# Between dilated attention and the RWKV recurrence: low-rank weights loaded with the constants, last statistics in three PSUM banks, memsets moved, first key norm ahead of the scan

## The reference

```python
for g, (window, dilation) in enumerate(((128, 1), (512, 4), (2048, 16))):
    num, den, mx = dilated_group_attention(q[g], k[g], v[g], ...)   # unnormalised
m_all = max(maxes); wts = [exp(mx - m_all) for mx in maxes]
o_attn = sum(w * n) / sum(w * d)                  # 8 heads of 64
y_attn = (o_attn * silu(z_attn)) @ w_up_attn
pr = pr + (pr_prev - pr) * shift_mix              # r, k, v, w_low, a_low
w_log = -softplus(-(w0 + tanh(w_low) @ w_up)) - 0.5
a = sigmoid(a0 + a_low @ a_up)
kk = k * k_k; kk = kk / max(norm(kk), 1e-12)      # per head: the key norm
k = k * (1 + (a - 1) * k_a)
y = rwkv7_scan(r, exp(-exp(w_log)), k, v, -kk, kk * a)
bonus = sum(r * k * r_k) * v
```

## Time and profile before

| | us |
|---|---|
| median of 3 runs | 2829.97 (2827.18 to 2830.27) |
| profiled execution | 2842.01 |
| span of the profiled execution | 2840.2 |
| TensorE matmuls busy | 2707.1 (95% of the span) |
| VectorE busy | 1264.2 (45%) |
| ScalarE busy | 810.1 (29%) |
| GpSimd busy | 1040.2 (37%) |

### The profile page before, as it was taken

How to read it: one execution, slowest core, us unless ns; L and a number is a source line. 1 busy time by engine, 2 the same in 40 slices (tenths; PEclk the granted TensorE clock), 3 DMA queues, 4 the chain that set the end, 5 groups by cost and what they waited for, 6 DMA issues and landing times.

```text
span 2840.2 us, 44277 instructions
## 1 busy us (share of the span) xinstructions
PE 2707.1 (95%) x17968; PEld 2176.6 (77%) x17968; DVE 1264.2 (45%) x2338; ACT 810.1 (29%) x1607; POOL 1040.2 (37%) x1318
## 2 busy tenths in 40 slices
PE   6999999997999999999898999999998998999999
PEld 5787777875867777686787888788887887777777
DVE  4225252435847466484531433533335003377743
ACT  3444444444113131220212211211113003255531
POOL 2223232232322231321455133344444456435442
PEclk9999999998999999999998899999999996999999
DMA  3111111111101010111331211111111121111122
GB/s 125 41 45 41 42 45 49 45 45 38 35 17 55 28 49 28 34 46 61 152 119 61 74 45 46 43 45 45 45 45 38 52 67 56 45 38 45 43 109 84
DMA packets 200907, 154.02 MB, mean 54 GB/s; under 512 B 5120, under 2 KB 183680, under 8 KB 200064
## 3 DMA queue, kind: packets, MB, share of 16 engines
q1 hardware_dynamic: 186256, 106.44, 12.6%
q10 hardware_dynamic: 14448, 44.74, 4.1%
HBM read 128.10 MB, written 23.07 MB: 53 GB/s over the span
## 4 chain that ended last, share of the span: by engine, by line
PE 79%; DVE 12%; ACT 6%; issue 1%; POOL 1%; DMA 1%; ACTq 0%; DVEq 0%; SPq 0%; POOLq 0%
PE gemm L527 21%; PE gemm L529 19%; PE gemm L528 19%; ACT prob L1942 3%; DVE neg_logits L1488 2%; DVE prob L1503 2%; PE scores L578 1%; PE scores L769 1%; PE weighted L829 1%; PE weighted L605 1%; PE probs_t L766 1%; PE probs_t L590 1%; PE scores L904 1%; PE scores L758 1%; DVE stats L1492 1%
## 5 line engine op out<-in xcount | busy, mean ns | idle before, releaser
L490 POOL CAST w_hi<-w_raw 128x512 fp32r<-128x512 f32 x360 | 249.1, 692 | 1686.8 <-PE gemm L529 1640.6
L527 PE MATMUL gemm<-h_hi,w_hi 128*128 128x512 f32 x1936 | 799.6, 413 | 9.7 <-ACT q_t L1702 7.6
L529 PE MATMUL gemm<-h_hi,w_lo 128*128 128x512 f32 x1936 | 761.9, 394 | 0.0
L528 PE MATMUL gemm<-h_lo,w_hi 128*128 128x512 f32 x1936 | 761.0, 393 | 0.0
L492 POOL TENSOR_TENSOR w_lo<-w_raw,w_hi 128x256 fp32r<-128x256 f32 x720 | 608.2, 845 | 56.9
L527 PEld LDWEIGHTS gemm<-h_hi,w_hi 128*128 128x128 f32 x1936 | 366.8, 189 | 102.8 <-issue 23.1
L529 PEld LDWEIGHTS gemm<-h_hi,w_lo 128*128 128x128 f32 x1936 | 366.8, 189 | 80.5
L528 PEld LDWEIGHTS gemm<-h_lo,w_hi 128*128 128x128 f32 x1936 | 367.6, 190 | 66.8 <-issue 1.9
L1382 DVE TENSOR_TENSOR scaled_product<-gemm,norm_rstd 128x512 f32<-128x512 f32 x116 | 80.2, 691 | 352.9 <-PE gemm L529 346.8
L527 PE MATMUL gemm<-xn_hi,w_hi 128*128 128x512 f32 x320 | 132.4, 414 | 7.2 <-POOL xn_lo L501 3.7
L1106 DVE CUSTOM_DVE_ANT_0 neg_logits<-scores,bias_tile 128x128 f32<-128x128 f32 (+1 forms) x192 | 67.6, 352 | 148.7 <-PE scores L578 142.9
(11 more groups left out here) (423 smaller groups left out, 4262.9 us busy)
## 6 DMA issues: line engine op xcount, KB each, us to landing
w_raw<-in_w_in SPq DMA_DIRECT2D x73, 512.0 KB, 3.9
w_raw<-in_a_w_in SPq DMA_DIRECT2D x48, 512.0 KB, 3.7
gates_scratch<-o_f ACTq DMA_DIRECT2D x32, 256.0 KB, 2.0
merge_gates<-gates_scratch ACTq DMA_DIRECT2D x4, 2048.0 KB, 15.1
w_raw<-in_a_w_out SPq DMA_DIRECT2D x16, 512.0 KB, 3.4
w_raw<-in_b_w_in SPq DMA_DIRECT2D x16, 512.0 KB, 3.7
x_rows<-in_x SPq DMA_DIRECT2D x8, 512.0 KB, 8.3
w_raw<-in_w_out SPq DMA_DIRECT2D x8, 512.0 KB, 3.4
```

What stands on the lines that cost most here:

```text
L490: Q(pool.tensor_copy(hi[:, ks, :], raw[:, s, ks, :]))
L527: pe.matmul(G[b][:], whi[:, s, k, :], hi(k, h), start=first, stop=False)
L528: pe.matmul(G[b][:], whi[:, s, k, :], lo(k, h), start=False, stop=False)
L529: m = pe.matmul(G[b][:], wlo[:, s, k, :], hi(k, h), start=False, stop=last)
```

## The change

- ScalarE issues the two loads of `lora_up` right behind those of the constants at the start of the kernel. They lie at 205.5 KB, into which `row_den` reached, so `row_den` moves from 204 to 202 KB.
- For pair 3 the four sets of statistics go to MB, to the two banks of S2, and to MB again. Set 3 waits only until set 0 is copied, sets 1 and 2 for the last quad's scores to be read (`ttr_done`). The first low-rank products wait until all sets are copied (`stat_in`).
- The memset of the last weights moves ahead of `best_of`, chunk_reset for pair 0 ahead of `mixed_in(3)`, and the two memsets in a_mats behind the eight products.
- For pair 0 the key norm's maximum goes ahead of r_k_products, its reciprocal ahead of the scan.
- The last attention output gets a semaphore of its own (`oa_last_out`); k_mod of pair 0 waits for the first three outputs, bonus for the last.

```diff
-        st_den = at("row_den", 204, [P, 8, 66])
+        st_den = at("row_den", 202, [P, 8, 66])
...
+        def stat_bank(p, j):
+
+            return (MB[:], S2[:, 0:HALF], S2[:, HALF:], MB[:])[j] if p == LAST else MB[:]
...
-                if 4 * p + j > 0:
+                if p < LAST and 4 * p + j > 0:
                     pe.wait_ge(E("stat_in"), 4 * p + j)
+                if p == LAST and j in (0, 3):
+                    pe.wait_ge(E("stat_in"), 4 * p if j == 0 else 4 * p + 1)
+                if p == LAST and j in (1, 2):
+                    pe.wait_ge(E("ttr_done"), len(quads))
                 for i in range(4):
-                    m = pe.transpose(MB[0:66, i * P:i * P + P], (st_max, st_den)[j // 2][:, 4 * (j % 2) + i, :], ident)
+                    m = pe.transpose(stat_bank(p, j)[0:66, i * P:i * P + P], (st_max, st_den)[j // 2][:, 4 * (j % 2) + i, :], ident)
...
                 pe.wait_ge(E("up_in"), 32)
+                if p == 0:
+                    pe.wait_ge(E("stat_in"), 4 * PAIRS)
...
                 if s in best_slots:
+                    if best_slots[s] == LAST:
+                        V(v.memset(weight[LAST][:].bitcast(F32), 0.0))
                     best_of(best_slots[s])
...
                 if s in weight_slots:
-                    if weight_slots[s] == LAST:
-                        V(v.memset(weight[LAST][:].bitcast(F32), 0.0))
                     weight_of(weight_slots[s])
...
+            V(v.memset(reset[:], 1.0))
+            V(v.memset(reset[:, 0:T:C], 0.0))
             mixed_in(3)
             for b in range(6):
                 blend(LAST, b)
-            for hh in range(2):
-                V(v.memset(AM[krows[hh], hh, :, 1, :], 0.0))
...
-                V(v.memset(reset[:], 1.0))
-                V(v.memset(reset[:, 0:T:C], 0.0))
+                if p > 0:
+                    V(v.memset(reset[:], 1.0))
+                    V(v.memset(reset[:, 0:T:C], 0.0))
+
+                def key_norm():
+
+                    dve.wait_ge(E("knorm_full"), p + 1)
+                    V(v.tensor_scalar(stat[:, 112:128], PV[:, 0:16], 1e-24, None, ALU.max), E("knorm_sb"))
+
+                def key_scale():
+
+                    dve.wait_ge(E("k_sqrt"), p + 1)
+                    V(v.reciprocal(stat[:, 112:128], stat[:, 112:128]), E("kinv"))
 
                 dve.wait_ge(E("k_gain"), p + 1)
+                if p == 0:
+                    dve.wait_ge(E("oa_out"), 16 * LAST)
                 V(v.tensor_tensor(kmod[:], kgain[:], rkT[:], ALU.mult))
+                if p == 0:
+                    key_norm()
                 V(v.scalar_tensor_tensor(rkr[:], rT[:], chan["rwkv_r_k"][:, one], kmod[:], ALU.mult, ALU.mult), E("rkr"))
+                if p == 0:
+                    key_scale()
...
-
-                dve.wait_ge(E("knorm_full"), p + 1)
-                V(v.tensor_scalar(stat[:, 112:128], PV[:, 0:16], 1e-24, None, ALU.max), E("knorm_sb"))
-                dve.wait_ge(E("k_sqrt"), p + 1)
-                V(v.reciprocal(stat[:, 112:128], stat[:, 112:128]), E("kinv"))
+                if p > 0:
+                    key_norm()
+                    key_scale()
...
                 if p == 0:
-                    dve.wait_ge(E("oa_out"), 16 * PAIRS)
+                    dve.wait_ge(E("oa_last_out"), 16)
...
+                if p == 0:
+                    for hh in range(2):
+                        V(v.memset(AM[krows[hh], hh, :, 1, :], 0.0))
...
             act.dma_start(pick_raw[:], d["shape_consts"][:, NCONST:NCONST + 2 * P]).then_inc(E("c_in"), 16)
+            act.dma_start(upw[0:64, :], d["rwkv_w_up"][0]).then_inc(E("up_in"), 16)
+            act.dma_start(upw[64:128, :], d["rwkv_a_up"][0]).then_inc(E("up_in"), 16)
...
-                A(a.activation(dst[32 * hn:32 * hn + 2, 0, :], MB[0:2, :], ACT.Copy))
-                src1 = MB[32:34, :].rearrange("p (r x q) -> p x r q", r=2, x=2)
-                src2 = MB[64:66, :].rearrange("p (r x l) -> p x r l", r=8, x=2)
+                bank = stat_bank(p, j)
+                A(a.activation(dst[32 * hn:32 * hn + 2, 0, :], bank[0:2, :], ACT.Copy))
+                src1 = bank[32:34, :].rearrange("p (r x q) -> p x r q", r=2, x=2)
+                src2 = bank[64:66, :].rearrange("p (r x l) -> p x r l", r=8, x=2)
...
-                act.dma_start(oA_d[p], numer[p % 2][:, 0, :]).then_inc(E("oa_out"), 16)
+                act.dma_start(oA_d[p], numer[p % 2][:, 0, :]).then_inc(E("oa_out" if p < LAST else "oa_last_out"), 16)
...
-            act.dma_start(upw[0:64, :], d["rwkv_w_up"][0]).then_inc(E("up_in"), 16)
-            act.dma_start(upw[64:128, :], d["rwkv_a_up"][0]).then_inc(E("up_in"), 16)
```

## The result

The median is 2816.4 us (2809.4 to 2821.0, 5 executions) against 2830.1 (2827.2 to 2843.1, 5) of the kernel before: ratio 0.9945 with the interval [0.9923, 0.9967]. The kernel is faster, by 14 us; 23 were forecast, and 2816.4 lies outside the range of 2802 to 2814. The profiled execution, however, took 2820.8 us against 2842.0, so 21.2 less, and 22.7 had been worked out for it. Both halves need an account: why the stretch came out nearly right, and where some 7 us of it (21.2 - 13.7) stay in the other executions.

A forecast was written before the change was run, and what follows sets the result against it. The stretch from about 635 to 730 us was taken as bound by latency, not matmuls. Gains of 23.3 us less 0.2, 0.1 and 0.3 gave 22.7: profiled 2819.3, median 2830.0 - 22.7 = 2807.3, range 2802 to 2814.

The forecast's parts named there:

- Step 1: Pair 3's statistics in three banks: TensorE no longer stalls, set 3 is copied at 650.1; gain 5.65 us.
- Step 2: After the statistics, the exponential no longer waits behind a late gemm half; gain 3.05 us.
- Step 3: The weight memset leaves the place between reciprocal and product for a time when VectorE waits; gain 1.73 us.
- contention: VectorE operations held back by GpSimd's splits, which move with the gemms; 0.3 us lost, range -0.5 to 1.5.
- Step 4: Low-rank weights loaded early, chunk_reset ahead of the last mix: first blend at 671.1; gain 5.3 us.
- Step 5: Memsets leave the place between the last blend and k_mod, which starts near 681.1; gain 3.7 us.
- rival (a): In the changed stretch, a low clock gives back part of the gain, 3 to 5 us: 2811; chance 0.14.
- Step 6: Pair 0's key norm ahead of the scan: spread at full clock, kk no longer waits; net gain 3.85 us.
- Step 7: Two a_mats memsets behind ak_ready, mostly covered by VectorE's wait for products; 0.2 us lost, at most 2.4.
- Step 8: At the kernel's start, two loads issued behind the constants cost 0.1 us, range 0 to 1.7.
- rival (c): Behind the products, the clock stays at half over pair 0's recurrence: slower, 2837 with 60 us of it; chance 0.03.
- every later stage earlier by the same: Sign in the profile behind the changed stretch: first products near 704.5, 23 us earlier, and all later stages likewise.

The follow-up runs named there:

- banks_only: Kernel before with only pair 3's statistics in three banks and their waits; 2820.7 us in one run, 85.5 us from copy of set 0 to masks.
- banks_loads: Kernel before with the three statistics banks plus early low-rank weight loads, moved row_den and split semaphore; 2814.2 us in one run, 80.0 us from copy to masks.
- norm_back: Changed kernel with pair 0's key norm back behind the scan; 2817.2 us in one run, 73.5 us from copy of set 0 to masks.
- after_exp: Changed kernel with the exponential's table loaded right behind the root, before ScalarE waits for the scan; 2811.1 us, ratio 0.9928.
- after_again: Changed kernel, unchanged, run once more; 2818.5 us, ratio 0.9945 to the kernel before.
- before_again: Kernel before, unchanged, run once more; 2834.4 us, ratio 1.0.
- before_delay11: Kernel before with 11 unread matmuls ahead of the last pass of an earlier gemm loop, delaying what follows 2.5 us; 2838.5 us, ratio 1.0014.
- after_delay4: Changed kernel with 4 unread matmuls ahead of the last pass of an earlier gemm loop, delaying what follows 0.9 us; 2812.7 us, ratio 0.9924.
- after_exp_warm: Changed kernel with the exponential's table loaded earlier and extra unread matmuls ahead of the two sum-of-squares stages; 2809.1 us, ratio 0.993.
- before_warm: Kernel before with 18 and 16 unread matmuls ahead of the two sum-of-squares stages; 2834.5 us, ratio 1.0002.

## Why the prediction was right in the trace and wrong in the median

First the steps, each against the trace after, then the step that failed.

- **Step 1** (5.65): right. Set 3 is copied at 650.35, predicted 650.1. No TensorE idle before the transposes.
- **Step 2** (3.05): right. The exponential starts 0.09 us behind the difference, at 653.73 (651.89 + 1.75 = 653.64). With banks_only steps 1 and 2 are worth 8.5 against 8.7.
- **Step 3** (1.73): the weights' high part ends at 666.09, predicted 665.6; the gain by then is 10.0 of 10.4 (0.2 went at set 3, 0.26 in the sums of denominators, see contention). The memset lies in idle time of VectorE (646.03).
- **Step 4** (5.3): right in the mechanism. First blend at 671.17, predicted 671.1, but that is partly luck: the step gave 5.7, which hides the 0.4 missing from step 3. banks_loads measures 5.6 for the loads alone.
- **Step 5** (3.7): k_mod starts 0.03 us behind the last blend, as said, but at 681.78, not 681.1. The blends took 10.58 us instead of 10.04: after the 2.80 us of idle time the clock fell for about 7 us and the spreads took 0.77 and then 0.63 us. That much of rival (a) came in the stretch, 0.5 us of its 3 to 5. Together the memsets of steps 3, 5 and 7 were undersized: undone they cost 6.2, not 4.3 (and not the 5.2 of the single terms), as the products then come late once more.
- **Step 6** (3.85): the place was right, the size wrong. The spread took 1.97 us, kk had no wait, but undoing the move costs 1.1 us. Its 3.85 held 1.7 us of half clock, and the sum counted them as the move's. They go without it: in norm_back the spread takes 1.97 us behind 2.78 us of idle time, whereas in banks_loads, without the moved memsets, it took 3.66 behind 6.49. And the step had the exponentials' table load as "now early". It is not: the load runs from 688.76, behind the wait for the scan, and the exponentials end at 693.30 instead of 691.4, so VectorE waits 0.88. after_exp takes this away, for 0.8. Which side of the wait a load stands on has to be read: the root's own load ran 8.8 us ahead of its activation before, by the timeline of ScalarE:

```profile
698.24 1.28 ACT L1763 ACT_TABLE_LOAD   x1 [0.86 <-ACT o_f L1739]
707.03 0.21 ACT L1763 ACTIVATE stats<-stats 128x16 f32<-128x16 f32 x1 [7.50 <-DVE stats L1231]
```

  The Trainium skill (ScalarE: Activation LUTs, section "What ACT_TABLE_LOAD costs") has 1283 ns for the load itself; the trace agrees (1.28). The same page (section "Step-by-step: what each stage is for") of the Trainium skill has the load placed right before its activation when the set isn't active; the rows at 688.76 and 690.05 in after agree, and step 6 overlooked it.
- **Step 7** (-0.2): the masks' 2.23 us of waiting became 0.29, so the cover was used up, as said.
- **Step 8** (-0.1): perhaps low, not shown. The load of pick_raw took 5.3 us from issue to landing instead of 4.9, and the first q_t evacuation came 0.4 us later in this pair of traces:

```profile
45.47 0.42 ACT L1704 ACTIVATE pick<-pick_raw 128x256 fp32r<-128x256 f32 x1 [5.68 <-DMA pick_raw<-in_shape_consts]
```

  But in after_again that load took 4.9 us again. Over all traces, the 12 with early loads are 0.3 us later at the q_t evacuation and 0.7 us later at set 0's copy than the 5 without (635.9 against 635.2); single traces of one kernel differ there by more than 1 us, so neither is clear of noise.
- **Contention** (-0.3): the product of denominators took 1.75 us, as before, though GpSimd was at work:

```profile
655.32 1.75 DVE L1138 TENSOR_TENSOR rows_den<-rows_den,rows_max 34x1536 f32<-34x1536 f32 x1 [1.68 <-ACT rows_max L1677]
```

  The 0.95 us by the rule of the Trainium skill (SBUF — State Buffer, section "SBUF: two separate sides") were not paid here, but the row is no test of it: the casts ran from 654.14 to 655.43 and so overlapped the product by 0.11 us at most, and GpSimd's spans are rough. The two sums of denominators behind it took 1.11 us each instead of 0.98, beside GpSimd's next split (655.51 to 660.77), and the term of 0.3 is close to these 0.26.
- **The sum**: 22.7 for the profiled execution; 21.2 came. The terms were 1.5 us too high in all, as the first products show (706.02, predicted 704.6). That the trace came this close holds some luck too: both profiled executions happened to have the same lengths of stage 1 (44.4, 44.5) and stage 2 (52.4, 52.5). Its own bounds add up to 8.0 us above 2807.3, more than the 2814 written, and even 2815.3 is below 2816.4.
- **The step that failed** is the last line of the sum's basis: "its difference is carried to the median unchanged", with its reason, "it moves as a block". The profiled execution of before lay 12 us above its median, that of after 4.4 (2820.8 - 2816.4). These 7.6 and the 1.5 of the terms are the 9.1 by which 2807.3 missed. The first figure stood in the text and was taken for an offset that both kernels share. Of the 12 us, 7.5 are a stage 1 that took 44.4 us instead of the 36.8 of before_again; the other 4.5 are open (stage 2 took 52.4 in all three traces of before, and 46.7 in before_delay11). And the average execution of the changed kernel loses about 5 us more to the clock outside the stretch than that of before. So the gain of the stretch is real, but it does not reach the median whole. The sign of this was to be had from the earlier trace rows: 20 us at clock 0.50 with TensorE busy throughout. It served for rival (c), a slower recurrence, which did not come (710 to 1480 us are at 0.99 as before), and should have served for a rival in which the gain is partly given back at those stages. Rival (a) named a low clock and 2811, but in the stretch.
- What was to show it ("every later stage earlier by the same") held in the first pair of traces (stage 2 begins 2355.66 and 2334.75, 20.9 apart; in before_again and after_again it is 15.7) and is not enough: one trace of each kernel says nothing of how its stages vary.

## What to carry to other kernels

- Before carrying a difference from one profiled execution to a median, ask how far the profiled one lies from its own median and which stage that distance is. If it is at a low granted clock with a busy TensorE, a shift of 1 to 4 us moved the mean loss here by 0 to 7 us, and a sum of 20 us needs that in its range.
- Where several steps each claim to remove a slow clock behind their own hole, count it once: with the other holes gone, step 6 was worth 1.1 us and not 3.85. A move past a table load has to say behind which wait the load stands; hoisting it (after_exp, 0.9928 [0.9914, 0.9943]) gave 0.8 us in the stretch. By ratio, after_delay4 (0.9924), after_exp and after_exp_warm (0.993) are the best versions run; their intervals overlap each other's and that of the changed kernel, so none is shown to be better, and the extra matmuls buy nothing that is shown on top.
- Each execution's span and mean clock part two causes that ratios mix: the rest (span x clock) is known to 0.2 to 1.2 us where the span scatters by 10.

## What was not expected of the hardware

- TensorE may be busy nearly all the time and still be granted 1.2 GHz: 20.0 of 20 us at 0.50 in the earlier trace rows, 35.2 of 37 at 0.71 in stage 1 of before. TensorE idled 6.80 us ahead of the first group of stage 1 in before, and groups of one-column matmuls alternate with gemm matmuls from there on. A low clock at the first group is not needed: in before_warm that of stage 2 is fast (2.03 us), and the later ones are slow behind 2.75 us of idle time. In all, 62 to 64 us of 2820 are lost to the clock, 2.2%, of which a change of place moves 5 to 7. The Trainium skill (TensorE: Matmul & The Clock Gate, section "Part 1: The HAM clock gate (the "warmup" mystery)") puts the penalty of the ramp, the first rise of the clock, at under 1% of a typical kernel's span; the 2.2% here are of falls all over the kernel, so they do not test that figure.
- The clock falls first between 40.0 and 43.6 us in all 17 traces, with TensorE idle (in before since 38.6 us). What the stages lose later depends on when they come, as the delays show for the changed kernel. Why 0.9 and 4.3 us help and 1.8 and 2.7 do not stays open.
- Raising the granted clock is not gaining time: before_warm lost 6.0 us less to the clock, its added work cost 6.6, and the kernel was no faster.
